# Two transformer blocks on one core: eleven instead of nine k-pairs of each down projection by seven products

## The chip, the core and the metric

The kernel runs on one core of a Trainium2 chip. The metric is the time of one execution on the device, in microseconds (us). Three runs of the kernel before took 2571.95, 2571.20 and 2571.33 us; their median, 2571.33, is the time before. All data are float32; TensorE multiplies in the float32r format.

## What is computed

Two transformer blocks in a row on one sequence of 256 rows of width 2048, each with a mixer and a feed-forward part. The change touches the down projections, the last matrix products of the two feed-forward parts:

```python
# first block
u_gate, u_val = jnp.split(u, 2, axis=-1)
x = x + (jax.nn.gelu(u_gate) * u_val) @ w_ffn_down[i]      # (256 x 5632) @ (5632 x 2048)
# second block
def swiglu(h, w_in, w_down):
    gu = h @ w_in
    gate, up = jnp.split(gu, 2, axis=-1)
    return (jax.nn.silu(gate) * up) @ w_down                # (256 x 5632) @ (5632 x 2048)
x = x + swiglu(rmsnorm(x, norm_ffn_g[layer]), w_ffn_in[layer], w_ffn_down[layer])
return rmsnorm(x, norm_final_g)
```

## The kernel before

The work runs in stages, one matrix product after the other: input projection, attention, output projection, up projection, down projection and gate of the first block, then the same kinds for the second. TensorE's instructions are written out in order; each engine has its own list, and semaphores (counters that one engine raises and another waits for) tie the lists together. Each float32 operand is split into a rounded part and a remainder, and each product is three matmuls (high by high, high by low, low by high; `block`, lines 1115 to 1117). ScalarE makes the rounded parts of the weights, VectorE the remainders.

**A down projection** has 44 k-tiles of 128, taken as 22 k-pairs (`PER_HALF`), and two halves of 1024 output columns. One k-pair of one half is a step, a "quad". A step multiplies two row blocks (tb) by two k-tiles by two column blocks of 512. Done plainly this is eight blocks of three matmuls (`eight`, an "8" in the patterns). Done by a Strassen-like scheme it is seven blocks (`seven`, a "7"): four of them with operands as they are, and three with sums of the stationary operands, against sums of the weight blocks. The patterns `EARLY` and `LATE` write out for each half in which order eights and sevens come. The first half of the first stage uses `LATE`, the other three halves use `EARLY`. Nine of the 22 are sevens in each half, and no two of them are neighbours.

**The ring SPL.** The split weight blocks stand in a ring of 11 slots (`SLOTS`), a slot holding the rounded part and the remainder of one 128x512 block. An eight takes one run of four slots. A seven takes a run of three (raw blocks) and a run of four (sums). `quads` (from line 156) hands out the runs: one that would pass the end begins at slot 0. It also notes for each run how many slot uses TensorE must have finished (`emptied`, counted by `q_used`) before it may be written. TensorE raises `q_used` by one behind each block of a seven, and by two at a time behind each half of an eight. It multiplies a seven in three groups, three blocks, two and two, each behind its own count of `q_lo`. The matmuls of a step therefore wait for `q_lo`, and the writers wait for `q_used`.

**What ScalarE and VectorE do for a step** (`roundings`, line 1632; `remainders`, line 2247). For an eight: ScalarE waits for the landed raw weights and `emptied[0]`, rounds four blocks (L1638); VectorE then subtracts (L2251). For a seven: ScalarE rounds three blocks (L1638); VectorE waits for `emptied[1]`, makes the four sums in three operations (L2258, L2260, L2262) in the remainder halves of the four-slot run, then the remainders of the three raw blocks (L2264, which lets TensorE begin the seven), then, behind ScalarE's two roundings of the sums (L1644), their remainders in two operations (L2269). Both engines work through the steps strictly in order.

**The raw weights** come in loads of 1 MB on SP's queue (`load_raw`, L605) into three entries; an entry is reloaded once the first remainders of the step that used it are made.

**The stationary sums** are made in the up projection by VectorE and ScalarE (tiles TR and SR), for 9 k-pairs (`SUM_J`) in five iterations (`SUM_ITS1`, `SUM_ITS2`), stored to DRAM by GpSimd (`sums_out`), and loaded in the down stage into STA, one place of 384 KB for each of the nine, beside the steps 2 to 10 (`load_sums`, L599). They stay there for both halves.

**At the end of a half** the products that are not yet in place are merged into X: ScalarE copies P1 once the last seven has been multiplied (`copy_p1`, L1649), then VectorE's `merge_first` (four operations, from L2280) behind the remainders of step 20 and `merge_second` (from L2291) behind those of step 21. In the second half of the first stage VectorE also makes the remainders PWL (L2378) of the next product's weights behind step 19. The last two steps of the fourth half are taken apart (from line 1368): six blocks of step 20, then step 21 is needed.

Of the kernel before, what the change touches and what calls it, by code (L numbers as in the profile page):

```python
# [12 lines left out]
F32 = mybir.dt.float32  # L13
F32R = mybir.dt.float32r
# [4 lines left out]
P = 128  # L19
# [4 lines left out]
NT = 512  # L24
# [173 lines left out]
SLOTS, ENTRIES = 11, 3  # L198
SUM_J = 9
PER_HALF = FKT // 2  # L200
EARLY, LATE = "8878787878787878787888", "8887878787878787878788"
ORDERS = [order_of(pattern, range(SUM_J), range(SUM_J, PER_HALF)) for pattern in (EARLY, LATE)]
QUADS = quads(((0, (ORDERS[1], ORDERS[0]), lambda n: (0, 0, 1)[n] if n < 3 else (0, 2, 1)[n % 3], True),
               (2, (ORDERS[0], ORDERS[0]), lambda n: n if n < 2 else (2, 1, 0)[n % 3], False)), SLOTS)
QUADS1, QUADS2 = QUADS[:2 * PER_HALF], QUADS[2 * PER_HALF:]
SUM_ITS1, SUM_ITS2 = 5, 5
PIN_J = 13
SUM_GROUPS = (range(0, 1), range(1, 2), range(2, 5), range(5, SUM_J))

# [11 lines left out]
def two_blocks_kernel(nc, x, p, norm_mix_w, w_in, rel_bias, w_gate_up, b_gate, gla_norm_w, w_out, norm_ffn_w,  # L221
# [3 lines left out]
    with ctx:  # L225
        def sem(name):
            return ctx.enter_context(nc.semaphore(name))
# [3 lines left out]
        def sb(name, shape, dt=F32, at=None):  # L231
# [8 lines left out]
            else:  # L240
# [93 lines left out]
        TRR = sb("TRR", [P, 2, 7 * P], F32R, at=o3 + 10240)  # L334
        STA = sb("STA", [P, SUM_J, 2, 3 * P], F32R, at=stationary)
        junk2 = sb("junk2", [P, NT], at=stationary + SUM_J * 6 * P * 4)
        ring = stationary + 32768
# [3 lines left out]
                sb("RAW22", [P, 2, 2 * NT], at=o3)]  # L341
        merge2 = sb("merge2", [P, NT], at=stationary + SUM_J * 6 * P * 4 + 2048)
        SPL1 = sb("SPL1", [P, SLOTS, 2, NT], F32R, at=ring + 4096)
# [117 lines left out]
        raw_in = [sem(f"raw_in{n}") for n in range(ENTRIES)]  # L461
        sum_in = [sem(f"sum_in{n}") for n in range(len(SUM_GROUPS))]
        q_hi, q_sum, q_lo, q_used = sem("q_hi"), sem("q_sum"), sem("q_lo"), sem("q_used")
# [33 lines left out]
        def sums_landed(q):  # L497
            n = [q.j in group for group in SUM_GROUPS].index(True)
            return sum_in[n], 16 * len(SUM_GROUPS[n]) * (q.half // 2 + 1)

# [32 lines left out]
        def _(sp):  # L533
# [64 lines left out]
            def load_sums(q):  # L598
                sp.dma_start(STA[:, q.j].rearrange("p h n -> p (h n)").bitcast(F32), sums_out[q.half // 2][q.j]  # L599
                             ).then_inc(sums_landed(q)[0], 16)  # L600

# [6 lines left out]
            for q in QUADS1:  # L608
                if q.n == 2:
                    sp.wait_ge(chunk_used, C_DOWN1)  # L610
                if q.n == 4:
                    sp.wait_ge(h_lo, 1 + 2 * (FF // NT))
                load_raw(w_down, q)
                if 2 <= q.n < SUM_J + 2:
                    load_sums([s for s in QUADS1 if s.seven][q.n - 2])
                if q.half == 1 and q.step == 12:
                    sp.wait_ge(q_used, multiplied_by(PER_HALF + 8))
                    for n in range(2):
                        sp.wait_ge(hi_done, C_PROJ + n - RING + 1)
                        sp.wait_ge(lo_done, C_PROJ + n - RING + 1)  # L620
                        sp.dma_start(PWR[:, n], rows(w_ple_proj, 0, slice(n * NT, (n + 1) * NT))
                                     ).then_inc(w_loaded[n], 16)
# [13 lines left out]
            for q in QUADS2:  # L636
# [9 lines left out]
                if n == 2:  # L646
                    sp.wait_ge(chunk_used, C_DOWN2)
                if 2 <= n < SUM_J + 2:
                    load_sums([s for s in QUADS2 if s.seven][n - 2])

# [10 lines left out]
        def _(pool):  # L661
# [88 lines left out]
            pool.wait_ge(hb_lo, 2 * (FF // NT))  # L750
            pool.wait_ge(q_used, multiplied_by(QUADS2[PER_HALF + 5].n))
            pool.dma_start(fw2[:], final_g2.partition_broadcast(P)).then_inc(sk_fg_in, 16)
# [3 lines left out]
        def _(pe):  # L756
# [365 lines left out]

            def sum_block(o, split, j, m, slot, begin, end):
                cols = slice((m - 2) * P, (m - 1) * P)
                return block(o, STA[:, j, 0, cols], STA[:, j, 1, cols], split, slot, begin, end)

# [12 lines left out]
            def seven(q):  # L1139

                sums, (p1, q5, p6, p7) = summands(q.half)
                j, s, t, split = q.j, q.slots[0], q.slots[1], split_of(q)
                pe.wait_ge(q_lo, q.split + 1)
                if q.half % 2 == 0:
                    pe.wait_ge(*sums_landed(q))
                raw_block(p1, split, 2 * j, 0, s, q.opens, q.ends).then_inc(q_used, 1)
                sum_block(sums[0][0], split, j, 4, s + 1, False, False).then_inc(q_used, 1)
                raw_block(sums[0][1], split, 2 * j + 1, 0, s + 2, False, False).then_inc(q_used, 1)
                pe.wait_ge(q_lo, q.split + 2)
                raw_block(q5, split, 2 * j, 1, t, q.opens, q.ends).then_inc(q_used, 1)  # L1150
                sum_block(p7, split, j, 3, t + 1, q.opens, q.ends).then_inc(q_used, 1)
                pe.wait_ge(q_lo, q.split + 3)
                sum_block(p6, split, j, 2, t + 2, q.opens, q.ends).then_inc(q_used, 1)
                mm = raw_block(sums[1][1], split, 2 * j + 1, 1, t + 3, False, False)
                mm.then_inc(q_used, 1)
# [1522 lines left out]
```

## Time and profile before

| | us |
|---|---|
| median of three runs | 2571.33 |
| the profiled execution | 2572.12 |
| its span, first to last instruction | 2570.2 |
| TensorE busy | 2559.9 |
| VectorE busy | 1693.3 |
| ScalarE busy | 1346.9 |
| first down stage (TensorE) | from 902.8 to about 1131 |
| second down stage (TensorE) | from 2333.8 on |

All rows are of this one execution. Its page gives sums over the whole span; the timeline gives the start of each instruction in us from the span's start, its duration in us, its engine, its line in the kernel (L...), what it writes and reads, and in brackets how long its engine had been idle before it and what ended that. Neighbours of one kind are merged into one row (x2). Matmuls overlap: each is shown with about 0.39 us, but they start every 0.227 us, and the distance of the starts is what counts. PE is TensorE's matmul stream and PEld its weight loads, DVE is VectorE, ACT is ScalarE, POOL is GpSimd, SP issues the weights' DMAs.

### The profile page before, as it was taken

To read this page: it belongs to the slowest core of one execution; us is meant where nothing else is said; L and a number is where in the kernel's file an instruction comes from. 1 tells how busy PE (TensorE), PEld (TensorE's weight loads), DVE (VectorE), ACT (ScalarE), POOL (GpSimd) and SP (SyncE) were. 2 spreads that over 40 slices of the span, in tenths; PEclk is the share of its full clock that TensorE was granted. 3 is DMA by queue.
4 is the path that set the end of the run, shared out by engine and by line. 5 is a ranking of instruction groups with operands and counts; after the bars stand their busy time and mean duration, and the time that the engine had idled before them with its cause. 6 is when DMAs were issued, how large, how long until landed. Compare 5 with 4: busy or idle time off the path is not lost.

```text
span 2570.2 us, 34530 instructions
## 1 busy us (share of the span) xinstructions
PE 2559.9 (100%) x12410; PEld 2131.0 (83%) x12410; DVE 1693.3 (66%) x2069; ACT 1346.9 (52%) x1729; POOL 99.6 (4%) x110
## 2 busy tenths in 40 slices
PE   9999999999999999999999999999999999999998
PEld 8887788888888888888887888888888888888887
DVE  6656556877777788875667565465555554547888
ACT  5455545666555554555645466434544444445454
POOL 2000000111111100000000000000000000000000
PEclk9999999999999999999999999999999999999999
DMA  7745555666665575655555545555566665657564
GB/s 242 220 149 156 165 188 172 215 206 206 189 188 190 167 284 196 225 184 187 186 172 156 164 154 158 194 190 183 177 209 198 215 197 187 193 186 255 203 216 161
DMA packets 281419, 493.82 MB, mean 192 GB/s; under 512 B 14578, under 2 KB 123236, under 8 KB 281056
## 3 DMA queue, kind: packets, MB, share of 16 engines
q1 hardware_dynamic: 277952, 478.73, 57.3%
q0 software_dynamic: 3184, 13.41, 1.6%
q8 instruction: 66, 1.08, 0.2%
q10 hardware_dynamic: 176, 0.27, 0.1%
q14 instruction: 41, 0.34, 0.0%
HBM read 483.17 MB, written 9.18 MB: 192 GB/s over the span
## 4 chain that ended last, share of the span: by engine, by line
PE 98%; DVE 1%; ACT 0%; issue 0%; DVEq 0%; ACTq 0%
PE acc L771 19%; PE acc L773 19%; PE acc L772 19%; PE acc L1071 13%; PE acc L1064 7%; PE tp L1115 3%; PE tp L1117 3%; PE tp L1116 3%; PE acc L1115 3%; PE acc L1117 3%; PE acc L1116 3%; PE tp L799 1%; PE tp L862 1%; PE tp L844 1%; PE tp L854 0%; PE tp L908 0%
## 5 line engine op out<-in xcount | busy, mean ns | idle before, releaser
L1941 DVE TENSOR_TENSOR WL<-WR,WH 128x1024 fp32r<-128x1024 f32 x712 | 882.7, 1241 | 704.6 <-ACT WH L1392 703.4
L1392 ACT ACTIVATE WH<-WR 128x1024 fp32r<-128x1024 f32 x712 | 754.0, 1059 | 878.1 <-PE acc L773 717.3
L771 PE MATMUL acc<-WH,A 128*128 128x512 f32 x1328 | 523.7, 394 | 0.4 <-DVE A L2009 0.3
L773 PE MATMUL acc<-WH,A 128*128 128x512 f32 x1328 | 517.5, 390 | 0.0
L772 PE MATMUL acc<-WL,A 128*128 128x512 f32 x1328 | 517.1, 389 | 0.0
L1071 PE MATMUL acc<-A,WH 128*128 128x512 f32 x1408 | 336.4, 391 | 0.0
L1071 PEld LDWEIGHTS acc<-A,WH 128*128 128x128 f32 x1408 | 258.6, 188 | 50.0
L771 PEld LDWEIGHTS acc<-WH,A 128*128 128x128 f32 x1328 | 249.4, 188 | 54.1 <-issue 4.0
L773 PEld LDWEIGHTS acc<-WH,A 128*128 128x128 f32 x1328 | 249.3, 188 | 53.0
L772 PEld LDWEIGHTS acc<-WL,A 128*128 128x128 f32 x1328 | 249.6, 188 | 49.7
L771 PE MATMUL acc<-WH,XH 128*128 128x512 f32 x544 | 216.4, 398 | 0.0
L772 PE MATMUL acc<-WL,XH 128*128 128x512 f32 x544 | 212.3, 390 | 0.0
L773 PE MATMUL acc<-WH,XL 128*128 128x512 f32 x544 | 212.2, 390 | 0.0
L1638 ACT ACTIVATE SPL<-RAW 128x1536 fp32r<-128x1536 f32 (+1 forms) x88 | 153.0, 1742 | 107.9 <-PE tp L1117 74.5
L1064 PEld LDWEIGHTS acc<-A,WL 128*128 128x128 f32 x1408 | 180.6, 191 | 6.9
L1064 PE MATMUL acc<-A,WL 128*128 128x256 f32 x1408 | 182.9, 283 | 0.0
L2251 DVE TENSOR_TENSOR SPL<-RAW,SPL 128x2048 fp32r<-128x2048 f32 x52 | 119.2, 2292 | 49.5 <-ACT SPL L1638 49.5
L1644 ACT ACTIVATE SPL<-SUM 128x1024 fp32r<-128x1024 f32 x72 | 76.5, 1062 | 101.1 <-DVE SUM L2258 87.2
L771 PEld LDWEIGHTS acc<-WH,XH 128*128 128x128 f32 x544 | 102.2, 188 | 23.0 <-issue 3.1
L773 PEld LDWEIGHTS acc<-WH,XL 128*128 128x128 f32 x544 | 102.1, 188 | 22.0
L772 PEld LDWEIGHTS acc<-WL,XH 128*128 128x128 f32 x544 | 102.2, 188 | 19.8
L1115 PE MATMUL tp<-SPL,BH 128*128 128x512 f32 x298 | 116.3, 390 | 0.4 <-DVE SPL L2264 0.3
(387 smaller groups left out, 3100.5 us busy)
## 6 DMA issues: line engine op xcount, KB each, us to landing
WR<-in_w_in_dram SPq DMA_DIRECT2D x199, 512.0 KB, 3.6
WR<-in_w_ffn_up_dram SPq DMA_DIRECT2D x176, 512.0 KB, 3.6
RAW<-in_w_ffn_down_dram SPq DMA_DIRECT2D x88, 1024.0 KB, 4.9
WR<-in_w_ffn_in_dram SPq DMA_DIRECT2D x176, 512.0 KB, 3.4
WR<-in_w_out_dram SPq DMA_DIRECT2D x64, 512.0 KB, 3.5
WR<-in_w_in_dram SPq DMA_DIRECT2D x65, 256.0 KB, 3.0
WR<-in_w_ple_gate_dram SPq DMA_DIRECT2D x32, 512.0 KB, 4.3
WR<-in_w_branch_a_dram SPq DMA_DIRECT2D x16, 512.0 KB, 3.7
```

The source lines that it names most:

```text
L771: pe.matmul(o, H[:, kt + k, cols], WH[:, s, k], start=begin, stop=False)
L772: pe.matmul(o, H[:, kt + k, cols], WL[:, s, k], start=False, stop=False)
L773: mm = pe.matmul(o, L[:, kt + k, cols], WH[:, s, k], start=False, stop=end)
L1064: mm = pe.matmul(acc[:, a, f, 0:T], low[:, k, f * P:(f + 1) * P], AH[:, 4 * q + k], start=False, stop=False)
L1071: mm = pe.matmul(acc[:, a, f, :], high[:, k, f * P:(f + 1) * P], both(kt), start=(kt == 0), stop=(kt == KT - 1))
L1115: pe.matmul(o, high, split[:, slot, 0], start=begin, stop=False)
L1116: pe.matmul(o, high, split[:, slot, 1], start=False, stop=False)
L1117: return pe.matmul(o, low, split[:, slot, 0], start=False, stop=end)
L1392: act.activation(WH[:, n % RING], WR[:, n % RING], ACT.Copy).then_inc(hi_done, 1)
L1638: act.activation(split[:, q.slots[0]:q.slots[0] + (3 if q.seven else 4), 0, :], blocks, ACT.Copy).then_inc(q_hi, 1)
L1941: dve.tensor_tensor(WL[:, n % RING], WR[:, n % RING], WH[:, n % RING].bitcast(F32), ALU.subtract).then_inc(lo_done, 1)
L2251: dve.tensor_tensor(split[:, s:s + 4, 1, :], raw, split[:, s:s + 4, 0, :].bitcast(F32), ALU.subtract).then_inc(q_lo, 1)
```

## The change

Eleven k-pairs of each half go by seven products, not nine. The two patterns are new; where sevens and eights alternated singly, they now hold places with two sevens in a row. The stationary sums are made for eleven k-pairs, in six iterations of the up stages. STA keeps its nine places but becomes a ring: a set is loaded for each seven of each half, 22 a stage, the first nine beside the steps 2 to 10 as before and each later one seven steps ahead of its use, behind a wait on SP for TensorE to be done with the seven nine sets earlier, and for the landing of the load four sets earlier on the same semaphore. TensorE waits for the landed set in every half, not in the first only. The gate of the load fw2 on GpSimd names its step by k-pair. The number of slots, the blocks and what ScalarE and VectorE do for one step are as they were.

```diff
...
 SLOTS, ENTRIES = 11, 3
-SUM_J = 9
+SUM_J, STA_SLOTS = 11, 9
 PER_HALF = FKT // 2
-EARLY, LATE = "8878787878787878787888", "8887878787878787878788"
+EARLY, LATE = "8878778787787877878788", "8887787877878778787788"
 ORDERS = [order_of(pattern, range(SUM_J), range(SUM_J, PER_HALF)) for pattern in (EARLY, LATE)]
 QUADS = quads(((0, (ORDERS[1], ORDERS[0]), lambda n: (0, 0, 1)[n] if n < 3 else (0, 2, 1)[n % 3], True),
                (2, (ORDERS[0], ORDERS[0]), lambda n: n if n < 2 else (2, 1, 0)[n % 3], False)), SLOTS)
 QUADS1, QUADS2 = QUADS[:2 * PER_HALF], QUADS[2 * PER_HALF:]
-SUM_ITS1, SUM_ITS2 = 5, 5
+SUM_ITS1, SUM_ITS2 = 6, 6
 PIN_J = 13
-SUM_GROUPS = (range(0, 1), range(1, 2), range(2, 5), range(5, SUM_J))
+SUM_SEMS = 4
+SEVENS = [[q for q in stage if q.seven] for stage in (QUADS1, QUADS2)]
 
...
-        STA = sb("STA", [P, SUM_J, 2, 3 * P], F32R, at=stationary)
-        junk2 = sb("junk2", [P, NT], at=stationary + SUM_J * 6 * P * 4)
+        STA = sb("STA", [P, STA_SLOTS, 2, 3 * P], F32R, at=stationary)
+        junk2 = sb("junk2", [P, NT], at=stationary + STA_SLOTS * 6 * P * 4)
-        merge2 = sb("merge2", [P, NT], at=stationary + SUM_J * 6 * P * 4 + 2048)
+        merge2 = sb("merge2", [P, NT], at=stationary + STA_SLOTS * 6 * P * 4 + 2048)
...
-        sum_in = [sem(f"sum_in{n}") for n in range(len(SUM_GROUPS))]
+        sum_in = [sem(f"sum_in{n}") for n in range(SUM_SEMS)]
...
         def sums_landed(q):
-            n = [q.j in group for group in SUM_GROUPS].index(True)
-            return sum_in[n], 16 * len(SUM_GROUPS[n]) * (q.half // 2 + 1)
+
+            k = (SEVENS[0] + SEVENS[1]).index(q)
+            return sum_in[k % SUM_SEMS], 16 * (k // SUM_SEMS + 1)
+
+        def sums_slot(q):
+            return SEVENS[q.half // 2].index(q) % STA_SLOTS
 
...
             def load_sums(q):
-                sp.dma_start(STA[:, q.j].rearrange("p h n -> p (h n)").bitcast(F32), sums_out[q.half // 2][q.j]
-                             ).then_inc(sums_landed(q)[0], 16)
+                k = SEVENS[q.half // 2].index(q)
+                landed, count = sums_landed(q)
+                if k >= STA_SLOTS:
+                    sp.wait_ge(q_used, multiplied_by(SEVENS[q.half // 2][k - STA_SLOTS].n))
+                if count > 16:
+                    sp.wait_ge(landed, count - 16)
+                sp.dma_start(STA[:, sums_slot(q)].rearrange("p h n -> p (h n)").bitcast(F32), sums_out[q.half // 2][q.j]
+                             ).then_inc(landed, 16)
+
+            def sums_beside(q):
+
+                for k, s in enumerate(SEVENS[q.half // 2]):
+                    behind = k + 2 if k < STA_SLOTS else s.n % (2 * PER_HALF) - 7
+                    if behind == q.n % (2 * PER_HALF):
+                        load_sums(s)
 
...
                 load_raw(w_down, q)
-                if 2 <= q.n < SUM_J + 2:
-                    load_sums([s for s in QUADS1 if s.seven][q.n - 2])
+                sums_beside(q)
                 if q.half == 1 and q.step == 12:
...
                     sp.wait_ge(chunk_used, C_DOWN2)
-                if 2 <= n < SUM_J + 2:
-                    load_sums([s for s in QUADS2 if s.seven][n - 2])
+                sums_beside(q)
 
...
             pool.wait_ge(hb_lo, 2 * (FF // NT))
-            pool.wait_ge(q_used, multiplied_by(QUADS2[PER_HALF + 5].n))
+            pool.wait_ge(q_used, multiplied_by([q.n for q in QUADS2 if q.j == SUM_J + 3][-1]))
             pool.dma_start(fw2[:], final_g2.partition_broadcast(P)).then_inc(sk_fg_in, 16)
...
 
-            def sum_block(o, split, j, m, slot, begin, end):
+            def sum_block(o, split, at, m, slot, begin, end):
                 cols = slice((m - 2) * P, (m - 1) * P)
-                return block(o, STA[:, j, 0, cols], STA[:, j, 1, cols], split, slot, begin, end)
+                return block(o, STA[:, at, 0, cols], STA[:, at, 1, cols], split, slot, begin, end)
 
...
                 pe.wait_ge(q_lo, q.split + 1)
-                if q.half % 2 == 0:
-                    pe.wait_ge(*sums_landed(q))
+                pe.wait_ge(*sums_landed(q))
+                at = sums_slot(q)
                 raw_block(p1, split, 2 * j, 0, s, q.opens, q.ends).then_inc(q_used, 1)
-                sum_block(sums[0][0], split, j, 4, s + 1, False, False).then_inc(q_used, 1)
+                sum_block(sums[0][0], split, at, 4, s + 1, False, False).then_inc(q_used, 1)
                 raw_block(sums[0][1], split, 2 * j + 1, 0, s + 2, False, False).then_inc(q_used, 1)
                 pe.wait_ge(q_lo, q.split + 2)
                 raw_block(q5, split, 2 * j, 1, t, q.opens, q.ends).then_inc(q_used, 1)
-                sum_block(p7, split, j, 3, t + 1, q.opens, q.ends).then_inc(q_used, 1)
+                sum_block(p7, split, at, 3, t + 1, q.opens, q.ends).then_inc(q_used, 1)
                 pe.wait_ge(q_lo, q.split + 3)
-                sum_block(p6, split, j, 2, t + 2, q.opens, q.ends).then_inc(q_used, 1)
+                sum_block(p6, split, at, 2, t + 2, q.opens, q.ends).then_inc(q_used, 1)
                 mm = raw_block(sums[1][1], split, 2 * j + 1, 1, t + 3, False, False)
                 mm.then_inc(q_used, 1)
```

## Rows read from the trace of the kernel before

**Rows 1.** The page: busy time and share of each engine; the chain that ended last.

```profile
PE 2559.9 (100%) x12410; PEld 2131.0 (83%) x12410; DVE 1693.3 (66%) x2069; ACT 1346.9 (52%) x1729; POOL 99.6 (4%) x110
...
PE 98%; DVE 1%; ACT 0%; issue 0%; DVEq 0%; ACTq 0%
```

**Rows 2.** Stretches: both down stages (columns in the first line).

```profile
core 0: us, PE busy (x) PEld busy (x) DVE busy (x) ACT busy (x) POOL busy (x), PEclk, DMA share, GB/s
902.00:1130.00 228.00, 227.60 (x1001) 186.96 (x1000) 193.14 (x162) 117.86 (x88) 2.06 (x2) 1.00 0.62 220
2334.00:2560.00 226.00, 225.43 (x994) 185.49 (x993) 192.12 (x161) 117.21 (x94) 0.55 (x1) 1.00 0.60 214
```

**Rows 3.** TensorE's waits: us in total, times, longest.

```profile
PE tp L1115 <- DVE SPL L2264: 0.3, 1, 0.3
...
PEld acc L1115 <- DVE SPL L2251: 0.7, 1, 0.7
...
PEld tp L1115 <- DVE SPL L2251: 0.4, 1, 0.4
```

**Rows 4.** Timeline of TensorE, first matmul of three steps: start us, us, what.

```profile
949.92 0.39 PE L1115 MATMUL acc<-SPL,BH 128*128 128x512 f32 x1
...
954.68 0.40 PE L1115 MATMUL tp<-SPL,BH 128*128 128x512 f32 x1
...
960.17 0.39 PE L1115 MATMUL acc<-SPL,BH 128*128 128x512 f32 x1
```

**Rows 5.** Timeline of VectorE over a seven and the eight behind it.

```profile
944.70 1.23 DVE L2258 TENSOR_TENSOR SUM<-RAW 128x1024 f32<-128x1024 f32 x1 [0.53 <-PE tp L1117]
...
947.30 1.75 DVE L2264 TENSOR_TENSOR SPL<-RAW,SPL 128x1536 fp32r<-128x1536 f32 x1
948.97 2.35 DVE L2269 TENSOR_TENSOR SPL<-SUM,SPL 128x1024 fp32r<-128x1024 f32 x2
952.13 2.29 DVE L2251 TENSOR_TENSOR SPL<-RAW,SPL 128x2048 fp32r<-128x2048 f32 x1 [0.81 <-ACT SPL L1638]
954.96 1.23 DVE L2258 TENSOR_TENSOR SUM<-RAW 128x1024 f32<-128x1024 f32 x1 [0.53 <-PE tp L1117]
```

**Rows 6.** Timeline of ScalarE: roundings of an eight and a seven, merged.

```profile
950.18 3.53 ACT L1638 ACTIVATE SPL<-RAW 128x2048 fp32r<-128x2048 f32 x2 [1.71 <-PE tp L1117]
```

**Rows 7.** Timeline of ScalarE, then VectorE, at the end of the first half.

```profile
1006.30 0.60 ACT L1649 ACTIVATE junk<-acc 128x512 f32<-128x512 f32 x1 [2.78 <-PE tp L1117]
...
1006.93 0.69 DVE L2280 TENSOR_TENSOR junk<-acc,junk 128x512 f32<-128x512 f32 x1 [1.09 <-ACT junk L1649]
...
1009.46 2.28 DVE L2251 TENSOR_TENSOR SPL<-RAW,SPL 128x2048 fp32r<-128x2048 f32 x1
```

**Rows 8.** Timeline of VectorE, then TensorE, at the last eight of all.

```profile
2553.11 2.29 DVE L2251 TENSOR_TENSOR SPL<-RAW,SPL 128x2048 fp32r<-128x2048 f32 x1 [0.68 <-ACT SPL L1638]
...
2554.76 0.39 PE L1117 MATMUL acc<-SPL,BL 128*128 128x512 f32 x1
2555.46 0.50 PE L1115 MATMUL acc<-SPL,BH 128*128 128x512 f32 x1 [0.31 <-DVE SPL L2251]
2555.80 0.40 PE L1116 MATMUL acc<-SPL,BH 128*128 128x512 f32 x1
```

**Rows 9.** Timeline of VectorE near the end of the first down stage.

```profile
1115.19 2.35 DVE L2378 TENSOR_TENSOR PWL<-PWR,PWH 128x1024 fp32r<-128x1024 f32 x2
```

**Rows 10.** Stretches of the up stages in which sums are made (columns as above).

```profile
400.00:600.00 200.00, 200.00 (x1149) 176.20 (x1148) 151.70 (x227) 123.85 (x173) 31.68 (x23) 1.00 0.64 199
...
1900.00:2100.00 200.00, 200.00 (x900) 165.94 (x899) 110.11 (x115) 94.59 (x108) 3.50 (x5) 1.00 0.65 207
```

**Rows 11.** DMA issues of 913:945, of 945:1000; ScalarE's timeline.

```profile
RAW<-in_w_ffn_down_dram SPq DMA_DIRECT2D x8, 1024.0 KB, 7.2
...
RAW<-in_w_ffn_down_dram SPq DMA_DIRECT2D x10, 1024.0 KB, 4.8
...
922.92 1.49 ACT L1638 ACTIVATE SPL<-RAW 128x1536 fp32r<-128x1536 f32 x1 [1.59 <-DMA RAW<-in_w_ffn_down_dram]
```

## The prediction

> **What bounds the kernel now.** I read the page first: TensorE is busy for 2559.9 of 2570.2 us, and it is 98% of the chain that ended last [rows 1]. Then the stretches: in both down stages TensorE is busy for all but half a microsecond at a granted clock of 1.00, while VectorE is busy 85% of the time [rows 2]. So taking matmuls away shortens the kernel, and whatever makes TensorE wait lengthens it. The waits of TensorE in these stages are few and short, and each names VectorE's remainders (L2251, L2264) [rows 3]. VectorE is then what comes next, and how close it is has to be read from one period of the ring SPL.
>
> TensorE's rows give the unit [rows 4]: a seven begins at 949.92, the eight behind it at 954.68, the next seven at 960.17. Seven blocks of three matmuls took 4.76, so a block is 0.68 us; eight of them are 5.44 (5.49 in the rows).
>
> VectorE's rows give the preparation [rows 5]. A seven starts its sums at 954.96, which is 0.28 behind 954.68, the end of the step two before it: the sums are written into the four-slot run, and that run is only free when that step has been multiplied. From the start of the sums (944.70) to the end of the first remainders (947.30 + 1.75 = 949.05) it takes 4.35; then TensorE may begin. The whole seven holds VectorE to 948.97 + 2.35 = 951.32, thus 6.6. An eight needs ScalarE's rounding first (from 950.18 [rows 6], VectorE at 952.13, so 1.95) and then 2.29.
>
> The slack follows. A seven behind an eight: 5.44 of matmuls cover 0.28 + 4.35 + 0.06 (from the end of the remainders to the matmul, 2555.40 to 2555.46 [rows 8]) = 4.69, 0.75 to spare. An eight behind a seven: 4.76 cover 0.28 + 1.95 + 2.29 + 0.06 = 4.58, 0.18 to spare. The alternation of before just fits the ring of 11 slots.
>
> **The gain.** Four halves have two sevens more each; every one saves one block of 0.68. 8 x 0.68 = 5.44 us, all on the path. Alone this is 2565.9.
>
> **The doubled groups.** The patterns hold 13 places with two sevens in a row (four in the order of the first half, three in each of the others), where before had none. Two sevens need 14 slots and the ring has 11, so the second cannot be made while the first waits. Walk the ring by the rule of `quads` (a run that would pass slot 11 begins at 0):
> - Kind A, nine places: the four-slot run of the second seven ends on the slot of the third block of the first. VectorE may start 0.28 after three blocks; TensorE has four left, 2.72. It needs 4.69. Wait: 4.69 - 2.72 = 1.97. (VectorE itself would be free sooner: it begins the first seven 5.16 before TensorE does, is done 6.6 later, 1.4 into it, and three blocks end at 2.04 + 0.28.)
> - Kind B, four places (slots 7 to 9, then 0 to 3): the run ends on the fourth block. Three blocks are left, 2.04: wait 2.65. The eight behind it has slots 4 to 7, the last of them the second seven's first block: rounding and remainders need 0.68 + 4.58 = 5.26 against 4.76, a further 0.50. Together 3.15.
>
> 9 x 1.97 + 4 x 3.15 = 30.3 us. Nothing gives it back: TensorE has no idle time elsewhere to recover.
>
> **The ends of halves.** The merge waits for the last seven. Where that is step 19, ScalarE copies P1 at 0.28 behind it, VectorE's first merge begins 0.63 later (1006.30 to 1006.93), takes 2.53 to 1009.46 [rows 7], and only then come the 2.29 of the last eight: 5.79 with 0.06, against 5.44. That is the 0.4 in [rows 3], and in before it stood at the end of the first half alone. The new order has it at the ends of all four. Third half: +0.35. Fourth half: TensorE takes only six blocks (4.08) of step 20 before it needs step 21, so the wait is 1.71; before waited 2555.46 - 2554.76 - 0.23 = 0.47 there [rows 8]: +1.24. Second half: VectorE also makes the two remainders PWL behind step 19 (2.35, less 0.08 that the next overlaps: 2.27 [rows 9]). Those stood behind an eight with room; now behind a seven: 1.4 + 2.27 + 2.29 + 0.06 = 6.0 after the seven's start against 4.76: +1.24, and the merge that follows is then hidden. Sum 2.8 us.
>
> **Starting again.** After its wait at 2555.46 the next matmul came 0.34 later, not 0.23 [rows 8]: 0.11 for each wait. 13 + 4 + 2 new ones make 2.1 us (bounds: 0, and 0.3 each, which is 5.7; I take the row).
>
> **What should cost nothing.**
> - The sums for two more k-pairs in the up stages, some 18 short operations on SR and TR more on VectorE and half as many on ScalarE: TensorE is busy for 200.00 of 200 us in stretches that hold such sums already [rows 10], with VectorE at 76 and 55%. Were that cover gone, I bound it by VectorE's own time, 5 us in all.
> - 26 more loads of stationary sums (384 KB) on SP's queue. Each stands behind a raw load, seven steps ahead of its use, and two stand in front of the next raw load at most. With a set beside each, raw loads landed in 7.2 us against 4.8 without [rows 11]. A raw load is issued when the first remainders of the step three before are out, which is 9.6 us or more ahead of its own use; 7.2 fits.
> - The new wait on SP is for a seven nine sets earlier. I counted steps: it is 15 to 19 before the one to be loaded, so 8 to 12 before the step beside which SP stands, and SP runs some 5 ahead of TensorE. It is long met. Behind it would stand the raw loads, so it would cost if it weren't; the wait for the landed set four earlier likewise. The moved gates of pin and fw2 stand on GpSimd, which has nothing else to do then.
> - TensorE's wait for a set in every half: landed by the above.
>
> **Sum.** -5.4 + 30.3 + 2.8 + 2.1 = +29.8. The profiled execution took 2572.12 us, 1.9 of it around its span of 2570.2: 2601.9 by it. The median of the runs, 2571.33, is 0.8 below that execution: 2601.1 us. About 0.2% (5 us) is what a measurement of this kernel can tell from no change.
>
> **Rivals.**
> 1. The ring's wait does not show, and only the fewer blocks do: 2565.9, just beyond 0.2% faster. It needs VectorE to prepare a second seven in 2.72 us; the break-even is a mean wait of 5.44 / 13 = 0.42 us a group. Against it: each remainder, each sum and each release in [rows 5] has the same length in all periods that I read, and the 0.18 and 0.75 of slack agree with waits of 0.3 to 0.7 exactly where the walk has them [rows 3]. 4%, and 1% for something between it and no change.
> 2. The waits are there but cheaper, as ScalarE and VectorE may close up where they now idle (VectorE idles 0.5 to 0.8 before each step). At half price: 2601 - 15 = 2586. 6%.
> 3. The change does less on SP than it says: 26 sets crowd the raw loads, so that these land after some 10 us and VectorE waits for them too. At 12 us each eight-seven pair would be 1 to 1.6 longer; some 20 pairs, about 22 us more: 2623. The first sets gave such a wait only once, 1.59 us, and on ScalarE alone [rows 11]. 3%.
> 4. TensorE's clock. So far its granted clock is 1.00 (2.4 GHz) in every stretch [rows 2, 10], but it has never idled for 2 us in this trace. If it fell to 1.2 GHz for the second seven of each group, seven blocks would cost 4.76 more each: 62 us, 2663. 3%. The Trainium skill ("TensorE: Matmul & The Clock Gate", section on a second HAM failure mode) reports a kernel in which brief idles between groups of matmuls made the clock swing between its levels; no stretch here shows that, and by that rule this rival would be the case.
>
> **The numbers.** The worked case has 83%. Its own range: without the cost of starting again and 0.3 less a group, 2595; with 0.3 for each restart and 3 us of unforeseen waits of the other engines, 2608. Eight in ten reaches a little into rival 2: 2592 to 2609. Faster by over 0.2%: 0.04; within 0.2%: 0.01; slower by over 0.2%: 0.95.
>
> **What would show it.** TensorE should have 24 matmuls fewer (12386), blocks of 0.68, and in the down stages some 15 us of waiting in each, released by L2264 thirteen times at about 2.0 or 2.65 us, by L2251 four times at 0.5, and 1.2 to 1.7 at the very last eight and the end of the first down stage. The up stages should be as long as before. ScalarE and VectorE should not wait for RAW, nor SP for TensorE. If L2264's waits are missing, the ring isn't what binds and the prediction falls; if VectorE waits for a DMA, rival 3; if a stretch has a granted clock under 1, rival 4.

## The result and the profile after

The changed kernel took 2604.62 us (median of 4 runs, 2603.05 to 2606.62), the kernel before 2571.64 beside it: a ratio of 1.0128, 95% interval 1.0113 to 1.0143. That is 33 us slower; forecast were 2601, range 2592 to 2609. The profiled execution took 2606.62 us, with a span of 2604.9 against 2570.2 of before.

The page after, as [rows 1]: busy us (share) and instructions of each engine, then the chain that ended last, by engine.

```profile
PE 2565.2 (98%) x12386; PEld 2129.3 (82%) x12386; DVE 1731.4 (66%) x2127; ACT 1363.8 (52%) x1753; POOL 103.2 (4%) x113
...
PE 95%; DVE 4%; ACT 1%; DMA 0%; issue 0%; DVEq 0%; SPq 0%; ACTq 0%
```

The 24 matmuls are gone (12410 to 12386), yet TensorE is busy for 5 us longer. In part that is how waits are counted: the last matmul ahead of one stands with its whole 0.39 us, where else 0.23 of it count. In part some matmuls have become slower. And 4% of the chain is now VectorE's.

The stretches after, as [rows 2] and [rows 10] (us; busy us and instructions of PE, PEld, DVE, ACT, POOL; granted clock; DMA share; GB/s):

```profile
902.00:1130.00 228.00, 212.95 (x910) 171.90 (x909) 192.90 (x166) 117.92 (x91) 2.07 (x2) 0.99 0.67 236
2334.00:2560.00 226.00, 213.32 (x919) 173.03 (x918) 186.75 (x159) 116.48 (x94) 0.55 (x1) 0.98 0.65 231
400.00:600.00 200.00, 200.00 (x1150) 176.25 (x1149) 151.70 (x228) 123.90 (x173) 31.69 (x23) 1.00 0.65 199
1900.00:2100.00 200.00, 200.00 (x904) 165.96 (x903) 114.77 (x122) 95.72 (x110) 2.94 (x4) 1.00 0.67 204
```

The up stages are as full as before. In each down stage TensorE now lacks some 13 to 15 us, and the granted clock is no longer 1.00.

TensorE's waits after, as [rows 3] (us in total, times, longest); L2280 are the remainders of a seven (L2264 before), L2267 those of an eight (L2251):

```profile
PE acc L1131 <- DVE SPL L2280: 19.9, 10, 2.5
PE tp L1131 <- DVE SPL L2280: 6.0, 3, 2.5
PE acc L1131 <- DVE SPL L2267: 3.1, 4, 1.4
...
PE tp L1131 <- DVE SPL L2267: 0.7, 3, 0.3
```

Thirteen waits for a seven's remainders, one for each doubled group. Here is one of kind A, VectorE first (start us, us), then TensorE:

```profile
979.16 1.23 DVE L2274 TENSOR_TENSOR SUM<-RAW 128x1024 f32<-128x1024 f32 x1 [0.89 <-PE tp L1133]
...
981.76 1.75 DVE L2280 TENSOR_TENSOR SPL<-RAW,SPL 128x1536 fp32r<-128x1536 f32 x1
```

```profile
981.39 0.39 PE L1133 MATMUL tp<-SPL,BL 128*128 128x512 f32 x1
983.56 0.50 PE L1131 MATMUL acc<-SPL,BH 128*128 128x512 f32 x1 [1.79 <-DVE SPL L2280]
983.90 0.40 PE L1132 MATMUL acc<-SPL,BH 128*128 128x512 f32 x1
...
984.60 0.44 PE L1132 MATMUL tp<-SPL,STA 128*128 128x512 f32 x1
984.84 0.63 PE L1133 MATMUL tp<-SPL,STA 128*128 128x512 f32 x1
985.27 0.63 PE L1131 MATMUL tp<-SPL,BH 128*128 128x512 f32 x1
...
987.83 0.58 PE L1131 MATMUL acc<-SPL,STA 128*128 128x512 f32 x1
988.24 0.39 PE L1132 MATMUL acc<-SPL,STA 128*128 128x512 f32 x1
```

VectorE idled until TensorE released the slot, took 4.35 from the start of its sums (979.16) to the end of the remainders (983.51), and TensorE went on 0.05 later. From 981.39 to 983.56 is 2.17; less the pace of 0.23 it is 1.94, forecast were 1.97. Then something that the forecast didn't have in this form: 1.3 us behind the wait the matmuls stand 0.43 apart instead of 0.23. The stretch around it (columns as above):

```profile
984.00:988.00 4.00, 4.00 (x13) 3.14 (x12) 3.98 (x3) 1.89 (x2) 0.00 (x0) 0.60 0.82 276
```

The granted clock is 0.60 on average there: the lower of its two levels, 1.2 GHz, for most of it, until 988.24. This happened behind four of the thirteen waits (from 927.03, 984.84, 2381.03 and 2531.28), each time for seven or eight matmuls in full and one or two at the edges in part (926.69 to 927.03 is 0.34). Each fall cost 1.6 us beyond the pace, edges included: 6.4 us. The other runs have fewer such falls, by their mean granted clock: 0.998 in the fastest (2603.05 us), 0.996 in this one.

So the 34.7 us by which the span is longer are, in us (the terms, each read by itself, come to 0.3 more):

| term | forecast | measured in the trace |
|---|---|---|
| eight blocks less | -5.4 | -5.4 |
| kind A, nine places | 17.7 (1.97 each) | 17.5 (1.94 or 1.95) |
| kind B, four places | 10.6 (2.65) | 10.5 (2.62 or 2.63) |
| the eight behind B | 2.0 (four of 0.50) | 1.4 (three of 0.46 or 0.47) |
| ends of halves | 2.8 | 2.5 (1.19, 1.59 less the 0.47 of before, 0.24) |
| starting again | 2.1 | 2.1 (0.10 or 0.11 each) |
| fallen clock | none | 6.4 (four of 1.6) |
| sum | 29.8 | 35.0 |

The fourth eight behind B, at 2535, had no wait: there the slowed matmuls gave VectorE the half microsecond. Where no clock falls (experiment 4), this eight waits 0.47 like the others.

### The profile page after: what moved, and what is told of

Read it like the earlier page. It is cut to its first block, busy times and chain, and to the rows that moved or that the text cites. A ratio compares the mean times of both kernels' runs of the same rounds, so it can differ in the third digit from the quotient of the medians.

```text
span 2604.9 us, 34562 instructions
## 1 busy us (share of the span) xinstructions
PE 2565.2 (98%) x12386; PEld 2129.3 (82%) x12386; DVE 1731.4 (66%) x2127; ACT 1363.8 (52%) x1753; POOL 103.2 (4%) x113
## 4 chain that ended last, share of the span: by engine, by line
PE 95%; DVE 4%; ACT 1%; DMA 0%; issue 0%; DVEq 0%; SPq 0%; ACTq 0%
PE acc L787 19%; PE acc L789 19%; PE acc L788 19%; PE acc L1087 12%; PE acc L1080 6%; PE acc L1131 3%; PE tp L1131 3%; PE tp L1133 2%; PE tp L1132 2%; PE acc L1133 2%; PE acc L1132 2%; DVE SPL L2280 1%; PE tp L815 1%; DVE SPL L2267 1%; PE tp L878 1%; DVE SUM L2274 1%
## 5 line engine op out<-in xcount | busy, mean ns | idle before, releaser
L1654 ACT ACTIVATE SPL<-RAW 128x2048 fp32r<-128x2048 f32 (+1 forms) x88 | 149.3, 1701 | 105.9 <-PE tp L1133 71.4
L1660 ACT ACTIVATE SPL<-SUM 128x1024 fp32r<-128x1024 f32 x88 | 93.4, 1062 | 114.1 <-DVE SUM L2274 97.1
L2267 DVE TENSOR_TENSOR SPL<-RAW,SPL 128x2048 fp32r<-128x2048 f32 x44 | 100.7, 2290 | 32.7 <-ACT SPL L1654 32.7
L1131 PE MATMUL acc<-SPL,BH 128*128 128x512 f32 x242 | 96.9, 400 | 23.3 <-DVE SPL L2280 19.9
```

Source lines behind the costliest of these rows:

```text
L1131: pe.matmul(o, high, split[:, slot, 0], start=begin, stop=False)
L1654: act.activation(split[:, q.slots[0]:q.slots[0] + (3 if q.seven else 4), 0, :], blocks, ACT.Copy).then_inc(q_hi, 1)
L2267: dve.tensor_tensor(split[:, s:s + 4, 1, :], raw, split[:, s:s + 4, 0, :].bitcast(F32), ALU.subtract).then_inc(q_lo, 1)
```

## Experiments

Beside each stands the kernel before on the same chip (2571.56 us for 1, 3, 4 and 5, 2571.48 for 2, 6, 7 and 8).

**1. All but the order.** The sums for eleven k-pairs, stationary sums loaded in every half (36 loads instead of 18), SP's new waits and the moved gate, but nine sevens a half in the patterns of before. (The eights of k-pairs 9 and 10 read operands over which sums have been written; the amount of work is that of before.)

```
-SUM_J, STA_SLOTS = 11, 9
+SUM_J, SEVEN_J, STA_SLOTS = 11, 9, 9
...
+EARLY, LATE = "8878787878787878787888", "8887878787878787878788"
-ORDERS = [order_of(pattern, range(SUM_J), range(SUM_J, PER_HALF)) ...
+ORDERS = [order_of(pattern, range(SEVEN_J), range(SEVEN_J, PER_HALF)) ...
```

> The changed kernel with the order of before: sums are made for eleven k-pairs, stored, STA is a ring of nine places that is reloaded through both halves behind its waits (18 loads a stage, with the two waits on SP and TensorE's wait in every half), but only nine k-pairs a half go by seven products, in the two patterns of before. The k-pairs 9 and 10 are multiplied by eight products although a part of their stationary operand has been overwritten by a sum, so that part of the result is another. Theory (the whole loss is the doubled groups in a ring of 11 slots): nothing of this costs anything, 2571.6 us within 1.5, TensorE's waits as before. Rival A (the loads, the waits on SP or the sums carry part of the loss): slower by 5 to 30 us, with VectorE or ScalarE waiting for RAW or SP for TensorE.

Measured: 2576.21 (2574.61 to 2577.77, 10 runs), ratio 1.0017 (1.0008 to 1.0027). A miss by some 4.6 us. Nearly all of it sits at one place. GpSimd, VectorE and TensorE in this kernel's timeline:

```profile
2499.90 0.55 POOL L768 DMA_DIRECT2D fw<-in_norm_final_g_dram  x1 [374.11 <-PE tp L1133]
```

```profile
2506.56 1.23 DVE L2619 TENSOR_TENSOR X<-X,fw 128x1024 f32<-128x1024 f32 x1 [2.91 <-DMA fw<-in_norm_final_g_dram]
```

```profile
2512.09 0.50 PE L1131 MATMUL acc<-SPL,BH 128*128 128x512 f32 x1 [2.56 <-DVE SPL L2280]
```

The change gates the load of fw2 (the final weights) behind the last use of k-pair 14, because fw2 now lies over those operands. In the order of before, k-pair 14 comes late: the load went out at 2499.90 instead of 2479.93, VectorE stood 2.91 us before its first product with fw2, TensorE waited 2.56 us for the seven behind it (2.72 beyond the pace), and its clock then fell, for 1.6 us more. In the changed kernel k-pair 14 comes earlier in the order; its load goes out at 2513.29, has landed at 2520.45 and is wanted only at 2535.36, so nothing waits.

**2. The same, with the gate of before.** The test of that reading.

```
-        fw2 = sb("fw2", [P, D], at=base + 2 * SUM_J * T * 4)
+        fw2 = sb("fw2", [P, D], at=base + 2 * SEVEN_J * T * 4)
...
-            pool.wait_ge(q_used, multiplied_by([q.n for q in QUADS2 if q.j == SUM_J + 3][-1]))
+            pool.wait_ge(q_used, multiplied_by(QUADS2[PER_HALF + 5].n))
```

> As the kernel with everything but the order, but with the load of the final weights fw2 at the place and behind the step of before (it lies over the operands of k-pairs 9 to 12 and waits for the step PER_HALF + 5 of the second down stage, as in before, instead of the last use of k-pair 14). In the trace of the kernel with everything but the order, GpSimd issued this load at 2499.90 instead of 2479.93, VectorE waited 2.91 us for it at its first product with fw2, TensorE then 2.56 us for VectorE's remainders, and its clock was at half for 3 us behind that. If that chain is the whole cost, this kernel is equal to before: 2571.6 us, within 1.0, with no wait of TensorE over 0.5 us in the down stages. If the 26 further loads or the sums for two more k-pairs cost the time, it stays at 2575 to 2577.

Measured: 2571.49 (11 runs) against 2571.48, ratio 1.0001 (0.9992 to 1.0010). So the sums for two more k-pairs, twice the loads of stationary sums (36 instead of 18) and SP's waits cost nothing, and a gate that was listed beside them can cost 4.7 us. (The changed kernel has 44 loads, eight more than this one; its ScalarE waited for raw loads 1.3 us in all.)

**3. Doubled groups alone.** The kernel before, nine sevens, with thirteen pairs of sevens next to each other.

```
-EARLY, LATE = "8878787878787878787888", "8887878787878787878788"
+EARLY, LATE = "8877887787877887878888", "8888778778877887787888"
```

> The kernel before with other patterns and nothing else: nine sevens a half as before, but in each half three or four places with two sevens in a row (13 in all, all of the kind where the run of the second seven ends on the third block of the first). No matmul is added or removed, no load and no sum. Theory: 13 waits of about 1.95 us for L2264 with 0.11 for starting again, 27 us, thus 2598.6, and 2 to 6 us more if TensorE's clock falls after some of the waits as in the changed kernel: 2598 to 2605. Rival A (loads, sums): 2571.6, as nothing of that has changed.

Measured: 2606.96 (2606.10 to 2611.22, 4 runs), ratio 1.0137 (1.0120 to 1.0154). The waits of its TensorE:

```profile
PE acc L1115 <- DVE SPL L2264: 18.7, 11, 2.1
PE tp L1115 <- DVE SPL L2264: 5.6, 4, 1.8
```

The order alone makes the whole loss, without any of the change's other parts. In its timeline thirteen waits stand beyond 0.5 us, eleven of them of 1.94 or 1.95 and two of 2.10 and 2.31, and the clock fell behind eight: 12.8 us in the profiled execution, the slowest of its four. The median is 2 us above the upper end of what was expected, which had room for 2 to 6 us of fallen clock; the mean granted clock of the other three runs, 0.995 or 0.996, fits four to six falls in each (the changed kernel's profiled execution, with four, has 0.996).

**4. The wait filled.** The changed kernel, with eight matmuls of zeros put into the same accumulator ahead of each second seven, where TensorE would wait. (The lines that place and write the zeros are left out.)

```
...
+                if QUADS[q.n - 1].seven:
+                    pe.wait_ge(zeroed, q.half // 2 + 1)
+                    for n in range(8):
+                        pe.matmul(sums[0][0], zeros[q.half // 2][:], BH[...], start=False, stop=False)
```

> The changed kernel with eight matmuls of zeros (128x128 of zeros by 512 columns, added to an open sum) ahead of the wait of each second seven: 1.8 us of work in waits of 1.95 and 2.63 us, so that TensorE does not idle there; the result is unchanged. GpSimd writes the zeros. Theory (the 3 us by which the changed kernel is above the forecast are the falls of TensorE's clock to half, four in the profiled run, each some 1.5 us): no fall, granted clock 0.999 or more, 2599 to 2602. Rival B (the falls cost nothing in the end, as the ring's waits shrink by what they take): 2604.6 within 1.

Measured: 2600.96 (2600.82 to 2602.11), span 2599.1, mean granted clock 0.999. One group of kind B in its timeline:

```profile
951.24 0.39 PE L1139 MATMUL tp<-SPL,BL 128*128 128x512 f32 x1
951.46 1.98 PE L1168 MATMUL tp<-BH,zeros 128*128 128x512 f32 x8
954.09 0.50 PE L1137 MATMUL acc<-SPL,BH 128*128 128x512 f32 x1 [0.65 <-DVE SPL L2291]
```

The useful matmul comes just as late (2.85 behind 951.24; in the changed kernel 2.86 at this place, 952.80 to 955.66), but no matmul in this trace is at half clock. Useless work makes the kernel 3.7 us faster (the ranges of the runs don't overlap), and its time is the forecast, which had no fallen clock, to 0.2 us. The spans, 2599.1 against 2604.9, agree: they differ by 5.8, the 6.4 of the four falls less the 0.58 that the eight at 2530.73 now waits and takes to start again. So the falls account for what the forecast missed.

**5. Remainders first.** The changed kernel, VectorE taking a seven's first remainders ahead of its sums: these write to the three-slot run, which is free earlier. Line L2280's operation moves up (not shown); SP's count of when RAW is free moves with it.

```
...
-                behind[e] = split + 1
+                behind[e] = split + (2 if seven else 1)
```

> The changed kernel, but for every seven VectorE makes the remainders of the three raw blocks first, which need only the three-slot run, and the sums behind them; a raw entry is reloaded one count of q_lo later. Theory by the same walk: the second seven of a doubled group is ready 1.3 us sooner (waits for L2264 of 0.6 to 0.7 instead of 1.95 and 2.63), but each seven now holds VectorE some 0.5 longer, since the roundings of the sums are waited for, and the eight behind a doubled group waits 1.4 to 1.5 for L2251, since VectorE's own work on 7-7-8 is more than TensorE's: in all 2600 to 2607, about as the changed kernel. If the ring's release were the only limit and VectorE's work no second one, the time would be 2578 to 2585. Rival A: 2604.6, with the waits where they are.

Measured: 2603.72 (2602.43 to 2604.62), ratio 1.0127 (1.0110 to 1.0144): no different from the change. TensorE's waits, L2285 being the remainders of the sums:

```profile
PE acc L1131 <- DVE SPL L2267: 16.0, 13, 2.4
PE tp L1131 <- DVE SPL L2285: 4.3, 9, 0.9
```

The wait of 1.95 has been cut in two: 0.59 within the second seven and 1.23 at the eight behind it, each with its 0.11. What binds is no longer what bound in the changed kernel, though. VectorE at the second seven of a doubled group here:

```profile
977.19 1.76 DVE L2272 TENSOR_TENSOR SPL<-RAW,SPL 128x1536 fp32r<-128x1536 f32 x1 [0.96 <-ACT SPL L1654]
978.86 1.22 DVE L2277 TENSOR_TENSOR SUM<-RAW 128x1024 f32<-128x1024 f32 x1
```

The first seven begins at 975.34, so the four-slot run of the second is free at 977.66 (three blocks, and the 0.28 of the prediction); its sums start only at 978.86, without an idle moment, right behind the first remainders. The same holds for all thirteen groups. Those remainders waited for ScalarE's rounding, and that (from 975.60) for the three-slot run. From there to the end of the remainders of the eight at 986.76 the two engines need 11.2 us, for which TensorE has 9.5 us of matmuls. So on this ring either order waits: one for the late four-slot run, the other for VectorE's and ScalarE's own work between the late three-slot run and the eight. The clock fell only once in this trace, behind its longest wait (2.60).

**6. A longer ring, in the order of the change.** SPL with 15 slots instead of 11, for which STA has four places instead of nine, each loaded anew when its set is used. (Some raw buffers also lie elsewhere, and the walk of a stage begins at slot 4 instead of 0; left out here.)

```
-SLOTS, ENTRIES = 11, 3
-SUM_J, STA_SLOTS = 11, 9
+SLOTS, ENTRIES = 15, 3
+SUM_J, STA_SLOTS = 11, 4
```

> The changed kernel with its own order, thirteen doubled groups and all, but with 15 slots of SPL instead of 11 (and four places of STA instead of nine). Theory: with 15 slots the second seven's run is free before the first is multiplied, its 4.35 us of preparation lie beside the eights ahead, and nearly all of the 30 us of waits go, the fallen clock with them: 2569.7 by the walk, range 2567 to 2574. If VectorE's work of 6.6 us a seven against 4.76 of matmuls were what makes the second seven late, most of the waits would stay: 13 x 1.4 to 1.8, 2585 to 2600.

Measured: 2574.71 (2574.16 to 2576.18, 10 runs), ratio 1.0013 (1.0004 to 1.0023), 0.7 above the range of the theory and far below that of the rival. Thirty of the 33 us are gone, with the same doubled groups and the same work. VectorE's rows for the second seven of a doubled group in the repaired kernel of 9 below, and the start of that seven on TensorE, whose first seven began at 2377.21:

```profile
2377.47 1.22 DVE L2275 TENSOR_TENSOR SUM<-RAW 128x1024 f32<-128x1024 f32 x1 [1.14 <-PE tp L1134]
...
2380.07 1.75 DVE L2281 TENSOR_TENSOR SPL<-RAW,SPL 128x1536 fp32r<-128x1536 f32 x1
2381.74 2.35 DVE L2286 TENSOR_TENSOR SPL<-SUM,SPL 128x1024 fp32r<-128x1024 f32 x2
2384.01 2.28 DVE L2268 TENSOR_TENSOR SPL<-RAW,SPL 128x2048 fp32r<-128x2048 f32 x1
2386.21 1.22 DVE L2275 TENSOR_TENSOR SUM<-RAW 128x1024 f32<-128x1024 f32 x1
```

```profile
2381.97 0.40 PE L1132 MATMUL acc<-SPL,BH 128*128 128x512 f32 x1
```

VectorE still waits for a slot before the second seven, for 1.14. But the slot is now freed by the eight ahead of the group, 0.26 into the first seven, and no longer by the third or fourth block of the first seven, 2.3 or 3.0 into it. The 4.35 of preparation from 2377.47 end at 2381.82, just before TensorE has multiplied the first seven. (The expectation had them beside the eights ahead; they lie beside the first seven, with 0.1 to spare.) From 2377.47 on VectorE goes from step to step without idling. In two of the thirteen groups (at 924.90 and 2521.03) it is not done with its earlier steps when the slot is free, and TensorE waits 1.0 us there.

**7 and 8. The longer ring with nine sevens, and with eleven in an order chosen for it.** The patterns of before in the one; in the other four patterns that a walk of the ring of 15 gave as the least waiting.

```
+PATTERNS = ('8887878787878787878788', '8878787878787878787888', ...            (nine)
+PATTERNS = ('8887877878778787787788', '8877878787877878778788',
+            '8877878778787787877888', '8877878778787877877888')                (eleven)
```

> Nine sevens a half in the patterns of before, sums for nine k-pairs; but the ring SPL has 15 slots instead of 11, paid for with five of the nine places of STA (four are left, each loaded anew when its set has been multiplied), and RAW11 and RAW21 lie elsewhere. It tells what the slots alone give. By the walk of the ring that the prediction used, the small waits of before go (0.3 to 0.5 us each): 1.6 us less than before, 2570.0, range 2569 to 2571.5. If the reloading of four places is late, it is over 2573.

> Eleven sevens a half as in the changed kernel, on a ring of 15 slots and four places of STA, and with patterns chosen by the walk (doubled sevens stand where the ring then holds both, five groups or fewer wait). Theory (11 slots don't hold two sevens, and a doubled group waits for that): the 8 saved blocks are kept, 5.4 us less than before: 2566.2, range 2565 to 2568.5. If doubled sevens cost for another reason (VectorE's work, the loads of sums), it is above 2575.

Measured: nine 2575.74 (ratio 1.0017, 1.0008 to 1.0026), eleven 2573.12 (1.0006, 0.9997 to 1.0015). Against the expected 2570.0 and 2566.2 they miss by 5.7 and 6.9 us, and both, like the kernel of 6, mostly for one wait near the end of the first down stage. In the kernel with eleven:

```profile
1123.52 0.39 PE L1134 MATMUL acc<-SPL,BL 128*128 128x512 f32 x1
1128.29 0.80 PE L1132 MATMUL acc<-SPL,BH 128*128 128x512 f32 x1 [4.38 <-DVE SPL L2268]
1128.89 0.63 PE L1133 MATMUL acc<-SPL,BH 128*128 128x512 f32 x1
```

`quads` puts the last run of this stage at the end of the ring, slots 11 to 14. In all three kernels the run before it had fallen on slots 11 to 14 or on 8 to 11, so the last one could not be prepared until that was multiplied. My walk had kept the place of the ring of 11 for it and did not see the clash. The wait, 4.54 beyond the pace, and the clock that fell behind it make 6.2 to 6.9 in the three traces.

**9. The last run freed.** In all three the last run but one goes to slot 0.

```
-                if at_end and half == len(orders) - 1 and i == len(order) - 1:
-                    at = slots - 4
+                if at_end and half == len(orders) - 1 and i >= len(order) - 2:
+                    at = slots - 4 if i == len(order) - 1 else 0
```

> As the kernel with eleven sevens on 15 slots, but the run of the last step but one of the first down stage is put at slot 0. In that kernel both of the last two steps had their run at slot 11 (the last has to be at the end of the ring), so the last one's rounding waited until the one before was multiplied: TensorE waited 4.38 us there and its clock was at half behind it; all together 6.7 us beyond the pace. If that is all that stood between the walk's 2566.2 and the measured 2573.1, this gives 2566.4, range 2565.5 to 2567.5: faster than before by 5 us. If the time was lost elsewhere too (the loads of sums, for which TensorE waited 0.55 us once), it stays over 2568.

> The changed kernel's own order on 15 slots, with the same repair of the last run. The kernel without it measured 2574.7, of which the clash at slot 11 took 6.5 in its trace. Theory: 2568.2, range 2567 to 2569.5; what is left beside the kernel chosen by the walk are two waits of 1.0 and one of 1.6 at the last eight. If the clash was only a part, over 2570.

> Nine sevens in the patterns of before on 15 slots, with the same repair. Without it: 2575.7, of which the clash took 6.6. Theory: 2569.1, range 2568.5 to 2570.5, the small waits of before gone (its gaps add up to 2.2 us). The difference to the kernel with eleven sevens on the same ring is then what the eight blocks of 0.68 bring, less the small waits that come with them: 2.5 to 4.

Measured, with the kernel before at 2571.60 beside them: eleven sevens in the chosen order 2566.80 (11 runs, 2566.12 to 2568.06), ratio 0.9982 (0.9973 to 0.9991); eleven in the order of the change 2568.73, 0.9989 (0.9980 to 0.9998); nine 2568.72, 0.9989 (0.9980 to 0.9998). All three within their ranges. The longest waits of the first kernel in the down stages:

```profile
PE acc L1132 <- DVE SPL L2281: 0.8, 1, 0.8
PE acc L1132 <- DMA STA<-sums_out: 0.5, 1, 0.5
```

It is faster than the kernel before, whose ratio's interval leaves 1 out. Its 11 runs also lie below all 11 of the nine sevens on the same ring and chip, by 1.9 us in the medians; as the interval of a ratio is some 2.3 us to either side, that size is rough. It is less than the 2.5 to 4 that was expected, and the two more sevens a half are not worth 5.4 here: the nine sevens on the long ring have 0.7 us of gaps left in the down stages, the eleven have 3.9 (the order of the change 5.6). VectorE is busy for 209.82 of 228 us there, against 192.71 with nine:

```profile
902.00:1130.00 228.00, 227.60 (x1003) 186.41 (x1002) 209.82 (x186) 123.51 (x97) 2.08 (x3) 1.00 0.70 246
```

```profile
902.00:1130.00 228.00, 227.81 (x1007) 188.12 (x1006) 192.71 (x164) 117.72 (x89) 2.07 (x2) 1.00 0.67 236
```

## Why the prediction was right, and where it was not

- **The walk of the ring** held to 0.03 us a wait: thirteen groups, nine of one kind and four of the other, at the places that it named. Experiment 3 shows that they alone make the loss, and experiment 6 that it is the 11 slots which make them, not VectorE's 6.6 us a seven: those are the same on 15 slots, where 30 us go. Experiment 5 shows that on 11 slots the other order of VectorE's work within a seven gains nothing; there the waits come from VectorE's and ScalarE's work behind the late three-slot run, so with that order this work does count.
- **The blocks saved**: 24 matmuls less in the trace. That eleven sevens pay is shown on the longer ring alone, and there for 1.9 of 5.4 us.
- **Starting again and the ends of halves** were sized right to 0.3 us together.
- **The term that failed is the clock.** It stood as a rival that was all or nothing: the second seven of every group at 1.2 GHz, 62 us, 3%. What came is a small form of it, seven or eight matmuls at the lower level behind four of thirteen waits, 6.4 us in the profiled execution, 3.7 in the medians (experiment 4). The likeliest case put it at nothing, though TensorE had never waited 2 us in this stage and no row said what that does to the clock; it should have been a term with bounds. That 2604.6 lies within the range all the same is in part luck: the room above 2601 was made for dearer starts (0.3 each, measured 0.11) and for other engines' waits, and neither came. The Trainium skill ("TensorE: Matmul & The Clock Gate", section "A second HAM failure mode: psum-queue depth-cycling") tells of a clock that swings where TensorE idles shortly between groups of matmuls. The trace agrees with that in kind; its size here is what the runs add.
- **What should cost nothing** did cost nothing (experiment 2). For the moved gate of fw2 the reason given, that GpSimd has nothing else to do, was no reason. What matters is when the load lands and who wants it; it holds in the changed kernel because 22 us lie between issue and use, and it fails with another order of the steps by 4.7 us (experiments 1 and 2).
- **Rivals 1 to 3** fell: the waits are there and at full price, raw loads landed in 5.2 us between 945 and 1000 and 5.8 between 913 and 945, and VectorE waited for no raw load.

Open: what decides behind which of the waits of 1.95 us the clock falls. The same wait, 1.94 us, had a fall behind it at 983.56 and none at 1112.84, and experiments that change only the history before one wait were not run.

## What to carry to other kernels

Before work is put closer together, walk the ring of its buffers with the release of each slot: a step that needs 7 slots twice in a ring of 11 waits for its predecessor's matmuls, however idle the engines are on average. A saved block of 0.68 us is worth nothing against one such wait of 2; space for four more slots, taken from a buffer that can be reloaded, brought more than the saved matmuls. When a buffer is moved to another place, look up what its load waits for in every order in which the steps may come.

## What the chip showed that I had not expected

- **Waits of 2 us cost more than their length.** Over all traces taken, TensorE's clock fell to 1.2 GHz for some 3 us behind 14 of 29 waits between 1.9 and 2.8 us (4 of 13 in the changed kernel, 8 of 13 in experiment 3, 1 of 2 in experiment 5, 1 of 1 in experiment 1), and behind the one of 4.5 us in each of three kernels. Each fall cost 1.6 us, and the one that lasted twice as long 2.3. Behind no shorter wait (up to 1.6 us, 28 between 0.5 and 1.6 in experiment 5) did it fall, nor with the waits filled by matmuls of zeros.
- **A slowed engine can hide a wait of its own:** the half microsecond at the eight behind a group of kind B was missing where the clock had fallen in the seven before.
